# First attention: probabilities turned by an ordinary product with the identity instead of by a PE transpose

## The chip, the cores and the metric

The kernel runs on one core of one Trainium2 chip. The metric is the device time of one execution in microseconds (us); lower is better. In the profile PE is TensorE (PEld its loads of weights), DVE is VectorE, ACT is ScalarE, POOL is GpSimd and SP is SyncE, which issues most transfers.

## The reference

Two transformer blocks on 256 tokens of 1024 features, in float32. The first has a mixer (attention with 8 heads beside a gated convolution) and a mixture of 32 experts; the second has a linear recurrence beside an attention with 16 heads, and an MLP. The change lies in the attention of the first block:

```python
def one_block(args):                      # a block of 128 queries
    qn_b, qr_b, s0 = args
    s = (jnp.einsum('bqhd,bkhd->bhqk', qn_b, k_nope) + jnp.einsum('bqhr,bkr->bhqk', qr_b, k_rope)) * ATTN_SCALE
    mask = (k_idx[None, :] >= PAD_FRONT) & (k_idx[None, :] <= q_idx[:, None])
    s = jnp.where(mask[None, None], s, NEG_INF)
    p = jax.nn.softmax(s, axis=-1).astype(v.dtype)
    return jnp.einsum('bhqk,bkhd->bqhd', p, v)
```

8 heads, 96 features of a query and a key (64 + 32 turned by position), 64 of a value; 16 meta tokens and 256 tokens are keys, the 256 tokens are queries.

## The kernel before

The program is written out by hand, engine by engine, and the engines meet at named semaphores. Weights come in slabs of 1 MB into a ring of 12 slots. ACT and DVE split each unit of a slab (128 x 1024) into a high and a low part (`WH`, `WL`, four buffers; the semaphore `unit_split`), PE multiplies with both and then frees the buffer (`unit_used`). A slot takes its first expert weights when the last unit of its slab is split.

First attention runs over steps n = 0 to 15, which are 8 heads times 2 blocks of queries (`qt` = n % 2). An even step has 144 keys (16 meta and 128), an odd step 272. Buffers alternate by n % 2. In each step:

- PE, `scores(n + 2)` (L1758): a product over 96 rows, into PSUM bank 4 or 5.
- DVE, `negative_max(n + 1)` (L1181 to L1183): adds the causal mask, takes the row maximum; then L1193 and L1194 divide the probabilities of step n by their sum (`prob_ready`).
- ACT, `exps(n + 1)` (L709): the exponent, with its sum; then L722 and L724 copy the turned probabilities of step n from PSUM to SBUF (`probT_ready`).
- PE, the turns (L1785, L1786): the probabilities of step n, queries by keys, become keys by queries in bank 6 or 7. An even step has one turn of 128 x 128 and one of 128 x 16, an odd step two of the first kind and one of the second (`prob_turned`).
- PE, `weigh_values(n - 1)` (L1770, L1771): the values of 128 keys, once or twice, and of the 16 remaining keys.

PE works in the order in which it is written: scores(n + 2), turns(n), values(n - 1). So each of its waits is for something that another engine has had about a step's time to do. `exps(n)` waits for the turns of n - 2. After step 15 PE waits for ACT's copies of the attention's result (`aT_ready`), and then multiplies with the output weights: the mix units, L1814 to L1816 in the helper `triple_rows`. Other names below: L1836 turns rows of tokens; L2088, L2121 and L2102 are the scores, turns and values of second attention, which has a like loop over 16 steps with two heads in each; L533 and L388 are where transfers are issued.

```python
for n in range(HEADS * TT):
    qt = n % TT
    if n + 2 < HEADS * TT:
        scores(n + 2)
    pe.wait_ge(ev("prob_ready"), n + 1)
```

Of the kernel before, what the change touches and what calls it, by code (L numbers as in the profile page):

```python
# [16 lines left out]
P = 128  # L17
# [3 lines left out]
META = 16  # L21
# [92 lines left out]
def build(nc, A, out):  # L114

    ctx = ExitStack()
    with ctx:
        def sb(name, shape, dt=F32):
            return ctx.enter_context(nc.sbuf_tensor(name, shape, dt))
# [31 lines left out]
        def ev(name):  # L151

            if name not in made:
                made[name] = ctx.enter_context(nc.semaphore(name))
            return made[name]
# [17 lines left out]
        ident = sb("ident", [P, P])  # L173
# [22 lines left out]
        ps = ctx.enter_context(nc.psum_tensor("ps", [P, 8, 512], F32))  # L196

        def ar(a, n, **k):
            return big[:, ARENA + a:ARENA + a + n]
# [17 lines left out]
        prob = ar(7424, 2 * T).rearrange("p (b t) -> p b t", b=2)  # L217
# [29 lines left out]
        def z(g):  # L247
            return big[:, Z0 + g * SLAB:Z0 + (g + 1) * SLAB].rearrange("p (c t) -> p c t", c=DC)

        zx, zg, zq, zk, _, _, zc, zi = (z(g) for g in range(8))  # L250
        g_lru, g_att, vtok2, ple = slot_tok(5), slot_tok(2), slot_tok(4), slot_tok(1)
        gain_final = big[:, Z0 + 7 * SLAB:Z0 + 7 * SLAB + D]
# [154 lines left out]
        def _(sp):  # L407
# [6 lines left out]
            for i, (name, _) in enumerate(SLABS1):  # L414
                if i >= RING:
                    sp.wait_ge(ev("unit_split"), LAST1[i - RING] + 1)
                s = slot((i + SHIFT1) % RING)
                if name in cols:
                    a, b = cols[name]
                    dst, src = s[:, 0:DC * (b - a)].rearrange("p (c n) -> p c n", c=DC), pcn(w_in)[:, :, a:b]  # L420
                elif name == "uq":
                    dst, src = s[:, 0:2 * 768].rearrange("p (c n) -> p c n", c=2), pcn(w_uq)
                elif name == "ukv":
                    dst, src = s[:, 0:D], w_ukv
                elif name.startswith("or"):
                    a = 256 * int(name[2:])
                    dst, src = s.rearrange("p (c n) -> p c n", c=2), pcn(w_out[a:a + 256, :])
                elif name in ("shg", "shu"):
                    w = A["w_sh_gate" if name == "shg" else "w_sh_up"][0]
                    dst, src = s.rearrange("p (c n) -> p c n", c=DC), pcn(w)  # L430
                else:
                    dst, src = s.rearrange("p (c n) -> p c n", c=2), pcn(A["w_sh_down"][0])
                sp.dma_start(dst, src).then_inc(slab1(i)[0], 16)
                if name == "or3":

                    sp.wait_ge(ev("split_low"), SP_AT["pre_mix"] + DC)
                    for k in range(TT):
                        sp.dma_start(h_tok[:, k, :], A["x"][0, k * P:(k + 1) * P, :]).then_inc(ev("h_loaded"), 16)
# [23 lines left out]
            def slot_empty(m):  # L462

                before_m = m - RING2
                if before_m == SLAB_LRU:
                    sp.wait_ge(ev("gates_done"), DC)
                else:
                    done = max(k for k, (mm, _) in enumerate(UNITS2) if mm == before_m) + 1
                    sp.wait_ge(ev("unit_split"), U1 + done)
# [1165 lines left out]
        def _(pe):  # L1635
            mm = nc.tensor.matmul
# [35 lines left out]
            tr = nc.tensor.transpose  # L1672
# [59 lines left out]
            b = uk % NB  # L1732
# [20 lines left out]
            def scores(n):  # L1753
                h, qt = divmod(n, TT)
                keys = META + (qt + 1) * P
                if n >= 2:
                    pe.wait_ge(ev("exp_done"), n - 1)
                mm(ps[:, 4 + n % 2, 0:keys], qcat[0:QD, h, qt * P:(qt + 1) * P], kcat[0:QD, h, 0:keys],  # L1758
                   start=True, stop=True).then_inc(ev("scores"), 1)
# [3 lines left out]
            def weigh_values(n):  # L1763
                h, qt = divmod(n, TT)
                pe.wait_ge(ev("probT_ready"), n + 1)
                o = ps[(h % 2) * VD:(h % 2 + 1) * VD, h // 2, qt * P:(qt + 1) * P]
                vs = slice(h * VD, (h + 1) * VD)
                pT = probT(n % 2)
                for k in range(qt + 1):
                    mm(o, vtok[:, k, vs], pT[:, k, :], start=k == 0, stop=False, skip_group_check=True)  # L1770
                mm(o, vtok[0:META, qt + 1, vs], pT[0:META, 2, :], start=False, stop=True, skip_group_check=True)\  # L1771
                    .then_inc(ev("att_out"), 1)
# [6 lines that stand above are left out]
                if n >= 2:  # L1779
                    pe.wait_ge(ev("probT_ready"), n - 1)  # L1780
                elif n == 1:
                    pe.wait_ge(ev("std_ready"), NORM_NO["conv"] + 1)
                b = n % 2
                for k in range(qt + 1):
                    tr(ps[:, 6 + b, k * P:(k + 1) * P], prob[:, b, k * P:(k + 1) * P], ident[:])  # L1785
                tr(ps[0:META, 6 + b, 3 * P:4 * P], prob[:, b, (qt + 1) * P:(qt + 1) * P + META], ident[:])\  # L1786
                    .then_inc(ev("prob_turned"), 1)
                if n:
                    weigh_values(n - 1)
            weigh_values(HEADS * TT - 1)  # L1790
# [207 lines left out]
            with pe.If(more > 0):  # L1998
                pe.wait_ge(ev("ffn_summed"), TT)
                pe.sem_inc(ev("o_by_tensor"), 1)  # L2000
                with pe.Fori(0, ROUNDS - 1) as r:
                    with pe.Fori(0, QUADS) as q:
                        b = r * QUADS + q
# [105 lines left out]
            for n in range(HEADS2):  # L2109
                j, qt = divmod(n, TT)  # L2110
# [146 lines left out]
```

## Time and profile before

| | |
|---|---|
| median of 3 runs | 1003.41 us (1003.18 to 1003.44) |
| the profiled execution | 1000.23 us, of which its span is 998.5 us |
| PE busy | 847.7 us, 85% of the span |
| DVE busy | 522.6 us, 52% |
| ACT busy | 384.9 us, 39% |
| granted TensorE clock, mean over the span | 0.911 of 2.4 GHz |
| read from HBM | 203.87 MB, 205 GB/s over the span |

A line of the profile names the engine, the line of the kernel, what is written and read, and the shape: `96*128 96x272` is a weight tile of 96 rows and 128 columns against 272 moving columns. `xN` counts records. An engine's row in 40 slices gives tenths of busy time in slices of 25 us each; PEclk there is the granted clock in tenths. In a table by stretch the columns are the stretch and its length, busy time of each engine with its number of records, then the granted clock, the DMA engines' share and GB/s. The chain of waits gives start, time until the next link, and what ran. A matmul's modelled end lies after the start of the next one, since they are pipelined, so in the timeline the time between two starts is what a matmul costs.

### The profile page before, as it was taken

How to read it: one execution, taken by the hardware profiler on the slowest of the kernel's cores; microseconds unless marked ns; L12 is line 12 of the kernel's file. 1: busy time of each engine (PE TensorE's matmuls, PEld its weight loads, DVE VectorE, ACT ScalarE, POOL GpSimd, SP SyncE). 2: the span in 40 equal slices, each digit the busy share in tenths (PEclk: the TensorE clock that was granted, in tenths of full speed). 3: DMA queues.
4: the chain of work that ended last, by engine and by line, in shares of the span. 5: the costliest groups of instructions: out<-in, count | busy, mean ns of one | idle time of the engine just before them, and what ended most of it. 6: DMA issues, size and time to landing. Idle time of an engine off the chain costs nothing.

```text
span 998.5 us, 13335 instructions
## 1 busy us (share of the span) xinstructions
PE 847.7 (85%) x5425; PEld 660.3 (66%) x5425; DVE 522.6 (52%) x857; ACT 384.9 (39%) x637; POOL 37.0 (4%) x101
## 2 busy tenths in 40 slices
PE   6878699878966777566799999769999999999975
PEld 3778455666633444223798987447787899889964
DVE  1669842464010101202675589885577666666655
ACT  3533533362100001003545575554534544444334
POOL 3000000000101101010000000000000000000000
PEclk9899855889988978888899999799999999999988
DMA  9941100614999999999750835206555556555101
GB/s 275 387 139 50 43 1 27 243 47 163 373 423 422 419 422 420 421 420 375 228 184 27 337 130 211 92 1 232 169 172 173 167 201 199 185 169 192 62 0 43
DMA packets 78287, 205.82 MB, mean 206 GB/s; under 512 B 8120, under 2 KB 51264, under 8 KB 65936
## 3 DMA queue, kind: packets, MB, share of 16 engines
q1 hardware_dynamic: 67584, 151.46, 42.4%
q0 software_dynamic: 8016, 53.27, 13.1%
q8 instruction: 45, 0.74, 0.3%
q10 hardware_dynamic: 2624, 0.20, 0.2%
q14 instruction: 18, 0.15, 0.0%
HBM read 203.87 MB, written 1.05 MB: 205 GB/s over the span
## 4 chain that ended last, share of the span: by engine, by line
PE 61%; DMA 16%; DVE 16%; ACT 4%; issue 2%; POOL 0%; SPq 0%; ACTq 0%; DVEq 0%
DMA big<-in_w_gate 14%; PE ps L1814 8%; PE ps L1815 8%; PE ps L1816 8%; PE ps L1640 7%; PE ps L1642 7%; PE ps L1641 7%; PE ps L1910 4%; DVE WL L1017 2%; DMA big<-in_w_in 2%; PE ps L1665 1%; DVE big L1499 1%; PE ps L1758 1%; PE ps L1770 1%; DVE WL L1009 1%
## 5 line engine op out<-in xcount | busy, mean ns | idle before, releaser
L1017 DVE TENSOR_TENSOR WL<-big,WH 128x1024 fp32r<-128x1024 f32 x154 | 186.7, 1224 | 110.6 <-ACT WH L601 109.2
L601 ACT ACTIVATE WH<-big 128x1024 fp32r<-128x1024 f32 x154 | 160.7, 1054 | 87.2 <-PE ps L1816 86.7
L1640 PE MATMUL ps<-XH,WH 128*128 128x256 f32 (+1 forms) x640 | 185.1, 289 | 5.9 <-DVE XL L1032 5.2
L1642 PE MATMUL ps<-XH,WL 128*128 128x256 f32 (+1 forms) x640 | 182.7, 285 | 0.0
L1641 PE MATMUL ps<-XL,WH 128*128 128x256 f32 (+1 forms) x640 | 182.6, 285 | 0.0
L1640 PEld LDWEIGHTS ps<-XH,WH 128*128 128x128 f32 x640 | 123.0, 192 | 9.1 <-issue 6.3
L1641 PEld LDWEIGHTS ps<-XL,WH 128*128 128x128 f32 x640 | 123.3, 193 | 0.8
L1642 PEld LDWEIGHTS ps<-XH,WL 128*128 128x128 f32 x640 | 123.2, 193 | 0.0
L1910 PE MATMUL ps<-big 128*32 128x256 f32 x1024 | 79.3, 478 | 51.5 <-DMA big<-in_w_gate 34.1
L1814 PE MATMUL ps<-WH,XH 128*128 128x512 f32 x256 | 103.9, 406 | 11.6 <-DVE WL L1009 5.0
L1910 PEld LDWEIGHTS ps<-big 128*32 128x32 f32 x1024 | 44.2, 137 | 88.9 <-issue 79.3
L1815 PE MATMUL ps<-WH,XL 128*128 128x512 f32 x256 | 101.9, 398 | 0.0
L1816 PE MATMUL ps<-WL,XH 128*128 128x512 f32 x256 | 101.6, 397 | 0.0
L1350 DVE TENSOR_TENSOR big<-big,ps 128x256 f32<-128x256 f32 x8 | 3.4, 421 | 130.7 <-ACT big L799 130.7
L1814 PEld LDWEIGHTS ps<-WH,XH 128*128 128x128 f32 x256 | 49.6, 194 | 25.5 <-DVE WL L1009 5.4
L1814 PE MATMUL ps<-WH,HH 128*128 128x512 f32 x144 | 57.1, 396 | 1.7 <-DVE HL L1596 1.7
L1815 PE MATMUL ps<-WH,HL 128*128 128x512 f32 x144 | 56.4, 392 | 0.0
L1816 PEld LDWEIGHTS ps<-WL,XH 128*128 128x128 f32 x256 | 49.3, 193 | 10.7
L1816 PE MATMUL ps<-WL,HH 128*128 128x512 f32 x144 | 56.1, 390 | 0.0
L1815 PEld LDWEIGHTS ps<-WH,XL 128*128 128x128 f32 x256 | 49.4, 193 | 9.9
L1009 DVE TENSOR_TENSOR WL<-big,WH 128x1024 fp32r<-128x1024 f32 (+1 forms) x39 | 40.2, 1044 | 21.8 <-ACT WH L592 21.5
L959 ACT ACTIVATE HH<-big 128x256 fp32r<-128x256 f32 x32 | 13.4, 417 | 76.2 <-DVE big L1593 76.2
(354 smaller groups left out, 1132.4 us busy)
## 6 DMA issues: line engine op xcount, KB each, us to landing
big<-in_w_in SPq DMA_DIRECT2D x35, 1024.0 KB, 9.2
big<-in_w_gate SPq DMA_DIRECT2D x16, 1024.0 KB, 16.5
big<-in_w_up SPq DMA_DIRECT2D x16, 1024.0 KB, 18.5
big<-in_w_gate POOLq DMA_DIRECT2D x16, 1024.0 KB, 18.7
big<-in_w_up POOLq DMA_DIRECT2D x16, 1024.0 KB, 20.7
big<-in_w_down SPq DMA_DIRECT2D x16, 1024.0 KB, 18.5
big<-in_w_down POOLq DMA_DIRECT2D x16, 1024.0 KB, 20.8
big<-in_w_mlp_up SPq DMA_DIRECT2D x16, 1024.0 KB, 5.5
```

The source lines that it names most:

```text
L601: s.activation(dst, src, ACT.Copy).then_inc(ev("unit_high"), 1)
L959: s.activation(HH[:, f % 2, :], zx[:, f % 2, :], ACT.Copy).then_inc(ev("relu_high"), 1)
L1009: v.tensor_tensor(dst, src, h.bitcast(F32), ALU.subtract).then_inc(ev("unit_split"), 1)
L1017: v.tensor_tensor(dst, src, h.bitcast(F32), ALU.subtract).then_inc(ev("unit_split"), 1)
L1499: ins = v.tensor_tensor_scan(out=cum(b)[:, h, S - keys:S][:, ::-1], data0=omb[:, h, ::-1], data1=ones[:, 0:1].to_broadcast([P, keys]), ini ...
L1640: mm(o, h, rh, start=first, stop=False, skip_group_check=skip)
L1641: mm(o, h, rl, start=False, stop=False, skip_group_check=skip)
L1642: return mm(o, l, rh, start=False, stop=last, skip_group_check=skip)
L1814: mm(o, h, WH[:, b, w], start=first, stop=False, skip_group_check=skip)
L1815: mm(o, l, WH[:, b, w], start=False, stop=False, skip_group_check=skip)
L1816: return mm(o, h, WL[:, b, w], start=False, stop=last, skip_group_check=skip)
L1910: last = mm(ps[j * CAP:(j + 1) * CAP, 1, up * FF:(up + 1) * FF], x(c)[:, j * CAP:(j + 1) * CAP], slot(first_slot + j)[:, c * FF:(c + 1) * FF],
```

## The change

The turns on L1785 and L1786 become ordinary products: the same operands (probabilities as the weights, the identity as what moves), the same place in PSUM, the same semaphore. The order of PE's instructions and every wait stay as they are. In what follows a turn is the transpose of one tile, a product the matmul that replaces it.

```diff
                 for k in range(qt + 1):
-                    tr(ps[:, 6 + b, k * P:(k + 1) * P], prob[:, b, k * P:(k + 1) * P], ident[:])
-                tr(ps[0:META, 6 + b, 3 * P:4 * P], prob[:, b, (qt + 1) * P:(qt + 1) * P + META], ident[:])\
-                    .then_inc(ev("prob_turned"), 1)
+                    mm(ps[:, 6 + b, k * P:(k + 1) * P], prob[:, b, k * P:(k + 1) * P], ident[:], start=True, stop=True)
+                mm(ps[0:META, 6 + b, 3 * P:4 * P], prob[:, b, (qt + 1) * P:(qt + 1) * P + META], ident[:],
+                   start=True, stop=True).then_inc(ev("prob_turned"), 1)
```

## Rows read from the trace of the kernel before

**Rows 1.** The page: PE's total, and three lines in 40 slices.
```profile
PE 847.7 (85%) x5425; PEld 660.3 (66%) x5425; DVE 522.6 (52%) x857; ACT 384.9 (39%) x637; POOL 37.0 (4%) x101
...
PEclk9899855889988978888899999799999999999988
DMA  9941100614999999999750835206555556555101
```

**Rows 2.** Busy time by stretch: one pair of steps, the stage, the first mix units.
```profile
149.37:155.31 5.94, 5.94 (x20) 3.43 (x19) 2.45 (x10) 1.89 (x8) 0.00 (x0) 0.50 0.00 0
124.30:170.40 46.10, 46.01 (x148) 25.99 (x148) 18.43 (x76) 15.93 (x64) 0.00 (x0) 0.50 0.00 1
...
171.80:175.50 3.70, 3.70 (x9) 2.94 (x10) 0.00 (x0) 0.65 (x2) 1.08 (x3) 0.50 0.73 263
```

**Rows 3.** The chain of waits through one pair of steps (start, us, what).
```profile
143.50 1.20 PE ps L1758 x2
144.71 0.43 PE ps L1785 x2
145.13 0.21 PE ps L1786
145.35 0.62 PE ps L1770 x2
145.97 0.61 PE ps L1771 x2
146.58 0.78 PE ps L1758 x2
147.36 0.21 PE ps L1785
147.57 0.21 PE ps L1786
147.79 1.04 PE ps L1770 x4
148.83 0.61 PE ps L1771 x2
```

**Rows 4.** Waits of SP's and POOL's queues, 120 to 240 us (total, times, longest).
```profile
SPq L388 <- DVE WL L1009: 118.0, 3, 82.3
...
POOL big L388 <- DVE WL L1009: 28.3, 2, 18.4
```

**Rows 5.** The chain of waits behind the last values.
```profile
170.41 1.39 issue
```

**Rows 6.** Groups by form on PE, 124.3 to 170.4 us (records, busy us, mean ns).
```profile
L1770 PE MATMUL ps<-XT,big 128*64 128x128 f32 x32 | 8.9, 435 | 0.0
...
L1785 PE MATMUL ps<-ident,big 128*128 128x128 f32 x24 | 8.7, 430 | 0.0
L1786 PE MATMUL ps<-ident,big 128*16 128x128 f32 x16 | 6.7, 421 | 0.0
...
L1770 PE MATMUL ps<-big 128*64 128x128 f32 x16 | 5.5, 448 | 0.0
```

**Rows 7.** By stretch: second attention twice, then before and after 482.7 us.
```profile
636.30:646.60 10.30, 9.34 (x44) 5.18 (x44) 8.94 (x20) 6.42 (x14) 0.00 (x0) 0.50 0.00 1
646.60:672.00 25.40, 17.68 (x150) 10.44 (x148) 23.50 (x50) 14.34 (x35) 0.00 (x0) 1.00 0.00 1
479.80:482.70 2.90, 2.84 (x14) 2.84 (x15) 0.92 (x3) 0.94 (x4) 0.00 (x0) 0.50 1.09 328
482.80:486.20 3.40, 3.18 (x26) 2.97 (x24) 3.26 (x8) 3.40 (x8) 0.00 (x0) 1.00 0.77 188
```

**Rows 8.** Timeline of PE around 482 us (start, us, instruction, idle before).
```profile
479.86 3.35 PE L1836 MATMUL ps<-ident,big 128*128 128x128 f32 x16 [10.07 <-DVE big L1415]
```

**Rows 9.** Timeline of PE in second attention.
```profile
658.93 0.44 PE L2102 MATMUL ps<-big 128*64 128x128 f32 x4
659.30 0.49 PE L2088 MATMUL ps<-big 64*128 64x128 f32 x4
```

## Prediction

> **What bounds the kernel now.** I read the page first. PE is busy 85% of the span, and its clock line stands at 5 tenths in the two slices from 125 to 175 us, where the line of the DMA engines is at 0 [rows 1]. This is the first attention, the stage that is changed. I then read the chain of waits through it: from 126 us to 170 us it runs almost wholly on PE, from one matmul to the next, with no step on DVE, ACT or DMA. The table by stretch agrees: from 124.3 to 170.4 us PE is busy 46.01 of 46.10 us, DVE 18.43, ACT 15.93, and the granted clock is 0.50 throughout, the lower of its two levels (1.2 GHz of 2.4) [rows 2]. So PE sets the time, at half its clock, and what is added to PE is added to the stage.
>
> The chain shows the rhythm [rows 3]. One pair of steps (an odd step, then an even one) takes 5.94 us: scores 1.20, two wide turns 0.43, the narrow one 0.21, values 0.62 and 0.61; then scores 0.78, turns 0.21 and 0.21, values 1.04 and 0.61. Sixteen steps make eight pairs.
>
> Does the rest shift with the end of this stage? SP's queue waited 118.0 us in three waits and POOL's 28.3 us for the split of weight units, which stands still until PE frees a buffer behind attention, and the DMA engines moved 0 to 1 GB/s meanwhile [rows 2, 4]. The expert transfers, which keep the DMA line at 9 from 250 to 475 us [rows 1], therefore start in step with the end of attention. Behind the last values comes a gap of 1.39 us for ACT's copies [rows 5], then the mix units. I count the shift one for one.
>
> **The change, part by part.** It takes away 40 turns (24 wide, 16 narrow, one record each) and puts 40 products in their place [rows 6]. Nothing moves in any engine's order, and no wait and no DMA is added. What does a product of 128 columns cost? The values are such products, in the same fp32. Eight even and eight odd steps hold 8 + 16 = 24 of them on line 1770, and the trace has 32 + 16 = 48 records [rows 6]: an fp32 product is issued as two passes, a turn as one. The pass costs the same either way: two further passes on line 1770 take 1.04 - 0.62 = 0.42 us, and two turns 0.43 [rows 3]. So each turn gains one pass of 0.213 us at the half clock. The weight load of the second pass lies under the first, as it does between the passes of line 1770, which follow without a gap; were it not so, each would cost as much as a change of shape, 0.62 - 0.43 = 0.19 us more. Below, the bound is nothing added (one pass after all).
>
> At the half clock that is 40 x 0.213 = **8.5 us** more. Nothing hides it: PE has 0.09 us idle in the stage. With unhidden loads it would be 16 us, which I count unlikely. A page of the Trainium skill speaks against the change: Perfetto Trace Analysis, section Transposes, says to use the transpose for a transpose and not an ordinary matmul. The rows agree as far as the price of a pass goes, and by that page alone the kernel would lose the 8.5 us.
>
> **The clock is the other term.** PE's stream in a pair is now 4.59 us of passes (5 turns; 10 of values at 0.213; scores 1.39) and 1.35 us of changes between groups of unlike shape, in which nothing streams. With the product it is 5.65 us of passes and the same 1.35, 7.0 us in all, and the passes added use all 128 rows of the array, unlike the scores (96) and half the values (16). The engine gets fuller; could the clock go up? Second attention has the same kind of loop: PE was busy 9.34 of 10.30 us at 0.50, and then the clock rose and stayed at 1.00 for 25.4 us in which PE was busy only 17.68 [rows 7]. So such a loop can lift the clock, and once lifted it is held by much less work than first attention offers. First attention as it is sits below what lifts it, not far below as I judge, since second attention looks little fuller.
>
> Does a turn count less than a product for the clock? Before 482.7 us PE ran sixteen turns and nothing else, at 0.50, and the clock then went to 1.00 [rows 7, 8]. Turns do lift it. The Trainium skill (TensorE: Matmul & The Clock Gate, section Part 4: PE-mode transpose) says that the full clock does not engage for transposes, which are not counted as PE being busy in the same way. The sixteen turns speak against that. Were the page right, the change would raise the counted work more than I say, and the rise below would be the surer.
>
> What a rise gives. From 124.3 to 170.4 us are 46.1 us; with the product at the half clock 54.6. At the full clock the passes of a pair take 5.65 / 2 = 2.83 us. The changes between shapes shrink less: in second attention two passes and such a change take 0.37 us at 1.00 (658.93 to 659.30) [rows 9], so 0.37 - 0.22 = 0.15 against 0.19. That gives 1.35 x 0.8 = 1.08, and a pair of 3.9 us; the ends are 3.5 (all halves) and 4.2 (changes stay). DVE (2.45) and ACT (1.89 us of work in a pair) [rows 2] still fit below it, and what they add in waits I put at 1 us over the stage, an estimate, for the first and last steps. With the rise t us into the stage it lasts t + (54.6 - t) x 0.56 = 30.6 + 0.44 t. I take t = 6: 33.2 us, 12.9 less than now. The first mix units, 3.7 us at 0.50 today [rows 2], would start at 1.00 and save 1.8. Less the 1 us: 13.7, say **14 us** saved. The profiled execution took 1000.23 us, 3.2 less than the median of 1003.41; I put the change on the median: **989.4 us**. Its own range is 984 (t = 0, a pair of 3.5) to 994 (t near 16).
>
> **The rivals.**
> *The clock stays at 0.50.* For it: 46 us of PE without a gap did not lift it, and the turns already counted. Against it: the passes go from 77% to 81% of the pair and gain full height. Price +8.5: 1012. It decides if the fuller loop is still not enough. Chance 0.33.
> *It rises late,* more than 16 us in. Each us later costs 0.44; the gain is used up at t of about 35 to 40. Times 994 to 1010. Chance 0.12, half of it faster, half slower.
> *The change does nothing to the end:* the product goes out in one pass, or the shift is taken up by the expert transfers. The two records of every product on line 1770 speak against the first, the waits of SP and POOL against the second. 1003.4, chance 0.05.
> *Forecast:* the clock rises in the first third. 0.50.
>
> **Numbers.** A measurement of this kernel can tell about 0.2% (2 us) from no change. Faster: 0.50 + 0.06 + 0.01 = 0.57; same 0.04; slower 0.33 + 0.06 = 0.39. Both signs hold much, so the range reaches from the forecast to the first rival: 986 to 1013.
>
> **What would show it.** In the profile after: 48 and 32 records where there were 24 and 16; the stage at 0.50 with a pair of 7.0 us, then at 1.00 with one near 3.9; the end of attention at about 157 us in place of 170, or 179 if the clock stays; SP's and POOL's waits shorter or longer by the same. It would be wrong if a clock that has risen falls back within the stage, if loads show as gaps between the two passes, or if the fast loop turned out to wait for DVE's max or ACT's exponent, whose time no clock of PE's changes.

## The result: the time and the profile after

The changed kernel takes 1013.8 us (median of 4 runs, 1012.9 to 1016.15) beside 1003.29 us before; the ratio is 1.0105, 95% interval 1.008 to 1.0131. It is slower by 10.5 us. The forecast was 989.4 us with a range up to 1013, so it had the wrong sign, and the time lies just outside the range. Now and then an execution falls into a slower state (one of the kernel before took 1594.82 us, one of burst_turns 1596.41, one of burst_one 998.31), and the medians and ratios below leave such executions out.

By stretch, the changed kernel: one pair of steps, the stage, the first mix units. They answer to [rows 2].

```profile
146.25:153.47 7.22, 7.22 (x25) 4.41 (x25) 2.45 (x10) 1.77 (x8) 0.00 (x0) 0.50 0.00 0
121.90:179.20 57.30, 56.74 (x188) 34.19 (x188) 18.87 (x78) 15.70 (x65) 0.00 (x0) 0.50 0.00 1
180.70:186.70 6.00, 6.00 (x14) 4.71 (x15) 0.00 (x0) 0.60 (x2) 1.03 (x2) 0.50 0.85 329
```

The granted clock (third number from the end) is 0.50 through the whole stage: the rise that the forecast stood on did not come. A pair takes 7.22 us in place of 5.94. The chain of waits of the changed kernel through that pair, link by link, against [rows 3]:

```profile
146.25 1.20 PE ps L1758 x2
147.45 0.85 PE ps L1785 x4
148.30 0.54 PE ps L1786 x2
148.84 0.62 PE ps L1770 x2
149.46 0.61 PE ps L1771 x2
150.07 0.78 PE ps L1758 x2
150.85 0.43 PE ps L1785 x2
151.28 0.54 PE ps L1786 x2
151.82 1.05 PE ps L1770 x4
152.86 0.61 PE ps L1771 x2
```

Scores and values are as they were. The wide products take 0.85 and 0.43 us where the turns took 0.43 and 0.21: one further pass of 0.213 each, as the prediction had it. The narrow ones take 0.54, not 0.43. The timeline of the changed kernel shows why.

```profile
147.88 0.42 PE L1785 MATMUL ps<-ident,big 128*128 128x128 f32 x1
148.23 0.13 PEld L1786 LDWEIGHTS ps<-ident,big 128*16 128x16 f32 x2 [0.23 <-issue]
148.23 0.61 PE L1786 MATMUL ps<-ident,big 128*16 128x128 f32 x2
```

The narrow product starts 0.35 us after the last wide pass and not 0.21: its weights are loaded only then (the row of PEld, its idle time before it given as "issue"), so a gap stands there as between the groups of unlike shape in [rows 3]. In the kernel before, the weights of the narrow turn are loaded under the last wide one, and it starts 0.21 us after it:

```profile
144.50 0.63 PE L1785 MATMUL ps<-ident,big 128*128 128x128 f32 x2
144.72 0.14 PEld L1786 LDWEIGHTS ps<-ident,big 128*16 128x16 f32 x1
144.93 0.42 PE L1786 MATMUL ps<-ident,big 128*16 128x128 f32 x1
```

The second pass of the narrow product comes a little sooner, and 0.11 us is left of the gap. In sum 40 x 0.213 = 8.5 and 16 x 0.11 = 1.8, together 10.3 us. From the first score to the last value, the start of the first record to that of the last, the stage takes 58.87 us in place of 48.11, 10.8 more. The other 0.4 us stand in its first and last steps, where the order of instructions isn't yet, or no longer, that of the steady part.

Behind it, SP's and POOL's queues wait longer for the same thing, as [rows 4] would have it after a longer stage:

```profile
SPq L388 <- DVE WL L1009: 127.7, 3, 92.6
...
POOL big L388 <- DVE WL L1009: 66.9, 3, 36.9
```

At the head of second attention the same instructions stand 10.4 us later than before (at 641.4 in place of 631.0 us), so the shift went through the expert transfers one for one. The profiled execution lies 14.3 us above the profiled one of before, and the other 4 us are those of second attention, in which the clock was down for 37.5 us this time, where it was down for 10.3 in [rows 7]:

```profile
644.10:681.60 37.50, 34.10 (x166) 19.52 (x166) 30.36 (x63) 20.64 (x46) 1.08 (x2) 0.50 0.02 8
```

Over the profiled kernels, this one included, second attention takes between 41.5 and 46.0 us with the same code, and the runs of one kernel spread by some us with it. So in what follows the stage is read in the trace, and the median only says how much of it arrives.

### The profile page after: what moved, and what is told of

It is laid out like the page before. It is cut to its first block, busy times and chain, and to the rows that moved or that the text cites. A ratio compares the mean times of both kernels' runs of the same rounds, so it can differ in the third digit from the quotient of the medians.

```text
span 1012.8 us, 13415 instructions
## 1 busy us (share of the span) xinstructions
PE 867.9 (86%) x5465; PEld 674.4 (67%) x5465; DVE 523.4 (52%) x857; ACT 384.9 (38%) x637; POOL 37.2 (4%) x101
## 4 chain that ended last, share of the span: by engine, by line
PE 64%; DMA 15%; DVE 14%; ACT 4%; issue 3%; POOL 0%; SPq 0%; ACTq 0%; DVEq 0%
DMA big<-in_w_up 15%; PE ps L1814 8%; PE ps L1815 8%; PE ps L1816 8%; PE ps L1640 7%; PE ps L1642 6%; PE ps L1641 6%; PE ps L1910 4%; DVE WL L1017 2%; PE ps L1889 1%; PE ps L1758 1%; PE ps L1770 1%; DVE XT L1459 1%; PE ps L2088 1%; PE ps L2121 1%
## 5 line engine op out<-in xcount | busy, mean ns | idle before, releaser
L1816 PEld LDWEIGHTS ps<-WL,XH 128*128 128x128 f32 x256 | 49.6, 194 | 10.8
```

The source lines that it names most:

```text
L1816: return mm(o, h, WL[:, b, w], start=False, stop=last, skip_group_check=skip)
```

## The experiments

Fourteen kernels. The stage is the time from the first score to the last value of first attention, a pair the distance of two odd steps in its steady part, both from the trace. The kernels ran in four sessions, each beside the kernel before: wide_only to narrow_full (before: 1001.46 us), burst_turns to r_products (1001.99), tall_products to burst_r_turns (1001.11), and the last two (1002.51). The kernel before differs by up to 2.2 us from session to session, so medians are compared with the one of their own session; the ratio does so, and it isn't always the quotient of the two medians. Stage, pair and clock are those of one profiled execution of each kernel. In each of the nine profiles marked 0.50 the clock was at 1.00 when the stage began and fell 1.9 to 2.4 us later.

| kernel | median us | ratio to before (95%) | stage us | pair us | clock in the stage |
|---|---|---|---|---|---|
| before | 1003.29 | | 48.11 | 5.94 | 0.50 |
| the change | 1013.80 | 1.0105 (1.008 to 1.0131) | 58.87 | 7.23 | 0.50 |
| wide_only | 1007.57 | 1.0059 (1.0043 to 1.0076) | 53.45 | 6.59 | 0.50 |
| narrow_only | 1007.67 | 1.0065 (1.0034 to 1.0095) | 53.48 | 6.59 | 0.50 |
| turns_twice | 1012.29 | 1.0108 (1.0089 to 1.0127) | 56.50 | 7.01 | 0.50 |
| narrow_full | (see text) | | 56.86 | 7.01 | 0.50 |
| burst_turns | 986.53 | 0.9830 (0.979 to 0.9869) | 32.49 | 3.49 | 1.00 from 124.9 to 152.2 |
| burst_products | 991.12 | 0.9885 (0.9852 to 0.9919) | 36.71 | 4.07 | 1.00 from 125.3 |
| r_turns | 998.74 | 0.9967 (0.9944 to 0.9989) | 44.13 | 5.41 | 0.50 |
| r_products | 1000.32 | 0.9979 (0.9954 to 1.0004) | 45.28 | 5.52 | 0.50 |
| tall_products | (see text) | | 35.15 | 3.79 | 1.00 from 129.0 |
| fuller_products | 994.38 | 0.9932 (0.9908 to 0.9956) | 40.38 | 4.52 | 1.00 from 128.6 |
| burst_one | 984.09 | 0.9812 (0.9771 to 0.9853) | 31.00 | 3.49 | 1.00 from 124.7 |
| burst_r_turns | 982.42 | 0.9799 (0.9771 to 0.9827) | 29.71 | 3.39 | 1.00 from 119.3 to 150.0 |
| fuller_low | 1019.19 | 1.0165 (1.0122 to 1.0209) | 65.70 | 8.08 | 0.50 |
| turns_more | 992.32 | 0.9889 (0.9848 to 0.9929) | 41.87 | 4.29 | 1.00 from 137.4 |

### What a product costs: four kernels

**wide_only**, against before:

```diff
-                    tr(ps[:, 6 + b, k * P:(k + 1) * P], prob[:, b, k * P:(k + 1) * P], ident[:])
+                    mm(ps[:, 6 + b, k * P:(k + 1) * P], prob[:, b, k * P:(k + 1) * P], ident[:], start=True, stop=True)
```

> Only the 24 wide turns become products; the 16 narrow ones stay turns. Theory of passes and shapes: each product adds one pass of 0.213 us at the half clock, 24 x 0.213 = 5.1 us, and no gap stands between the wide product and the narrow turn if the gap of 0.11 us seen with the change belongs to a narrow product; if it belongs to a change from a product to another width, 16 x 0.11 = 1.8 us come on top (6.9). Rival theory, that the product as such and not its second pass is dear: the price would not be in step with the number of passes. Clock at 0.50 through first attention in both. Whole kernel 1003.3 + 5.1 to 6.9 = 1008.4 to 1010.2 us.

The pair grew by 0.65 us, which is three passes (0.64), so no gap stands between a wide product and a narrow turn.

**narrow_only**: the narrow turn alone becomes a product, as in the change.

> Only the 16 narrow turns become products. Theory of passes and shapes: 16 x 0.213 = 3.4 us, and the 0.11 us gap in front of each stays if it is the narrow product that cannot have its weights loaded ahead: 16 x 0.32 = 5.2 us. If the gap needs a product before it, 3.4 us alone. Whole kernel 1006.7 to 1008.5 us.

The pair grew by 0.65 us again, now for two products: 0.32 each, 0.213 for the pass and 0.11 for the gap. The gap belongs to the narrow product, be it a wide turn or a wide product that stands before it. The two halves add up: 5.34 + 5.37 = 10.71 us in the stage, against 10.76 for the change.

**turns_twice**, against before: both turn lines issued twice.

```diff
                 for k in range(qt + 1):
                     tr(ps[:, 6 + b, k * P:(k + 1) * P], prob[:, b, k * P:(k + 1) * P], ident[:])
+                    tr(ps[:, 6 + b, k * P:(k + 1) * P], prob[:, b, k * P:(k + 1) * P], ident[:])
```

> The kernel before with each of the 40 turns issued twice, so that PE makes as many passes as with the products, but all in transpose mode. The result is the same. If the price is the pass alone: 40 x 0.213 = 8.5 us, and no gap between wide and narrow, so 1.8 us less than the change: about 1011.8 us. If the array's clock took turns for less work than products, nothing differs, since the clock is at 0.50 in both. A rival that the product has a price of its own beyond the pass would leave this run well under the change by more than 1.8 us.

7.01 is 5.94 + 5 x 0.213: a second turn costs what the second pass of a product costs, and there is no gap. That the product has a price beyond its second pass and the narrow one's gap is ruled out. The median lies 10.8 us above that of before, where the stage grew by 8.4; second attention took 3.1 us more in this profile.

**narrow_full**, against the change:

```diff
-                mm(ps[0:META, 6 + b, 3 * P:4 * P], prob[:, b, (qt + 1) * P:(qt + 1) * P + META], ident[:],
+                mm(ps[:, 6 + b, 3 * P:4 * P], prob[:, b, (qt + 1) * P + META - P:(qt + 1) * P + META], ident[:],
```

> The changed kernel, with the narrow product widened: its weight tile is 128 columns that end with the 16 remaining keys, not those 16 alone. The rows that are then copied are of other keys, so the output is not the reference's. It keeps the number of passes (80) and takes away the change of width between the wide and the narrow product. If the gap of 0.11 us is due to that change, 16 x 0.11 = 1.8 us less than the change, about 1012.0 us; if it is due to the second product's weights being loaded late whatever their width, no difference (1013.8 us).

With weights of equal width the pair is 7.01 us, 0.22 less than with the change: the gap is gone. It came from the change of width from 128 to 16 columns in front of a narrow product; in front of a narrow turn the same change costs nothing. The median, 4482 us, can't be compared: with other attention values the kernel runs its overflow rounds, which it needs only when an expert gets more tokens than it has room for, and 3936 us lie between the two attentions in place of 461.

### What an extra burst of work at the head of the stage does

In the profile of the kernel before, the clock is at 1.00 when the stage begins, at 121.9 us, and falls at 124.3, when PE has waited 1.5 us for the first exponents. In the stretch ahead of the fall PE is busy 1.17 of 3.40 us:

```profile
120.90:124.30 3.40, 1.17 (x5) 0.54 (x4) 3.03 (x7) 0.44 (x2) 0.00 (x0) 1.00 0.00 0
```

**burst_turns**, against before:

```diff
             scores(0)
             scores(1)
+            for _ in range(2):
+                mm(ps[:, 3, :], ones[:], vtok[:, 0, :], start=True, stop=True)
```

> The kernel before, with two extra products of 128 x 512 (four passes) written into a PSUM bank that is not yet in use, placed behind the first two scores of first attention, where PE idles 1.5 us until the first exponent is done. Their result is never read. Theory: the clock falls at the start of the stage because PE runs dry there, and once at 1.00 it would be held by the loop, as second attention holds it. Then the stage runs at 1.00: a pair of steps about 3.5 us in place of 5.94, attention 14 to 16 us shorter, whole kernel about 988 us. Rival: the loop of first attention holds no clock, or it falls later all the same: within 2 us of 1003.3, or part of the gain.

The busy time by stretch: the burst, then the rest of the stage.

```profile
120.90:124.80 3.90, 3.90 (x7) 2.31 (x8) 3.03 (x9) 1.05 (x4) 0.00 (x0) 0.50 0.00 0
124.90:152.10 27.20, 26.08 (x145) 15.22 (x143) 17.61 (x72) 14.95 (x61) 0.00 (x0) 1.00 0.00 1
```

In this profile the clock was at 0.50 already when the scores and the burst began, at 120.9 us. PE ran without a gap for 3.90 us, the clock went to 1.00, and the loop of turns held it there for 27.2 us. The stage lost 15.6 us and the kernel 15.5. So the loop that 46 us at 0.50 had not lifted holds the clock once something else has lifted it. The burst need not find the clock down: in the profile of burst_r_turns below it was at 1.00 from 119.3 us, before the stage began, and stayed there.

**burst_products**: the same two lines in the changed kernel.

> The changed kernel with the same two extra products behind the first two scores. If the clock is held at 1.00 a pair takes about 3.9 to 4.1 us (in place of 7.2), the 40 second passes cost 40 x 0.11 = 4.4 us at the full clock, and the kernel is 4 to 5 us above the run with turns and extra products, about 993 us. Rival, that the clock falls all the same: 1013.8 us.

Here a pair is 4.07 us; at the full clock the change costs 0.58 us a pair, 4.2 us in the stage and 4.6 in the median, less than half of its 10.5 at the lower clock.

**burst_one**: one such product in place of two.

> The kernel before with one extra product (128 x 512, two passes) behind the first two scores in place of two. If it is only PE's dry stretch at the head of the stage that has to be filled, half of it still leaves a gap of about 0.7 us: the clock then stays at 0.50, a pair at 5.94 us and the time at 1002 us, or within 1 us. If any work there is enough, it is as with two: pairs of 3.5 us and about 987 us.

My expectation was wrong: one is enough, and it saves 1.5 us of the stage besides. It had reckoned with a burst at the full clock. In this profile the clock was at 0.50 at that point, the burst of one took 1.71 us, and PE went on without a gap until the clock had risen. One of its 4 runs was at 998.31 us, the others at 982.64 to 984.47, so it may not catch every time; that run was not profiled.

### Rounded operands

**r_turns**, against before:

```diff
+        prob_r = sel_flat[:, 0:2 * T].rearrange("p (b t) -> p b t", b=2)
+        ident_r = sel_flat[:, 6 * P:7 * P]
...
-                v.tensor_scalar(prob[:, b, 0:keys], prob[:, b, 0:keys], small[:, 10 + b:11 + b], None, ALU.mult)\
+                v.tensor_scalar(prob_r[:, b, 0:keys], prob[:, b, 0:keys], small[:, 10 + b:11 + b], None, ALU.mult)\
...
-                    tr(ps[:, 6 + b, k * P:(k + 1) * P], prob[:, b, k * P:(k + 1) * P], ident[:])
+                    tr(ps[:, 6 + b, k * P:(k + 1) * P].bitcast(F32R), prob_r[:, b, k * P:(k + 1) * P], ident_r)
```

> The kernel before, but DVE writes the scaled probabilities as rounded fp32r (into the space of the keys' high and low parts, free by then) and the turns are of fp32r with an fp32r identity. The probabilities lose low bits. If a turn of fp32r streams one column a cycle, where fp32 takes two, 40 x 0.107 = 4.3 us less at the half clock: about 999 us. If a turn takes the same whatever the type, 1003.3 us.

5.41 = 5.94 - 5 x 0.107: an fp32r turn takes half the time of an fp32 one.

**r_products**: fp32r operands in the changed kernel, with `mm` in place of `tr`.

> The changed kernel with the same fp32r probabilities and identity: an fp32r product goes in one pass of one cycle a column, as in the rest of the kernel (0.107 us for 128 columns at the half clock). Theory of passes: 40 x 0.107 = 4.3 us less than before, plus up to 16 x 0.11 = 1.8 us for the change of width: 999 to 1001 us, and 12 to 15 us under the change. Rival, that a product with the identity is dear whatever its type: near 1013.8 us. The probabilities lose low bits.

One pass of 0.107 us, like the fp32r turn, plus the gap of the narrow product, 2 x 0.055 a pair: 5.52. In fp32r the product loses to the turn by the gap alone, so most of what makes the change dear is fp32's second pass. The median can't be told from that of before. The chain of waits of r_turns shows the narrow turn at 0.11 us:

```profile
150.13 0.21 PE ps L1788 x2
150.35 0.11 PE ps L1789
```

**burst_r_turns**: both ideas together, in case they beat both kernels.

> The two extra products and the fp32r turns together. The clock as with the extra products alone; each of the 40 turns takes 0.055 us in place of 0.109 at the full clock, so up to 2.2 us less than the run with the extra products alone, if PE and not DVE or ACT still sets a pair of 3.49 us: about 985 us, ratio to before near 0.981. If another engine sets it by then, no difference. The probabilities lose low bits.

982.42 us, ratio 0.9799 (0.9771 to 0.9827): 2% under before and 3% under the change. A pair is 3.39 us, 0.10 less than with fp32 turns where the passes would give 0.27: in the steady part PE is busy 17.89 of 19.00 us, where in burst_turns it was 19.59 of 20.00 (130 to 150 us), so PE no longer sets all of it.

```profile
130.00:149.00 19.00, 17.89 (x107) 11.16 (x107) 12.99 (x53) 10.91 (x45) 0.00 (x0) 1.00 0.01 2
```

### What was missing for the clock to rise

The forecast had the second pass lift the clock. **fuller_products**, against the change:

```diff
                     mm(ps[:, 6 + b, k * P:(k + 1) * P], prob[:, b, k * P:(k + 1) * P], ident[:], start=True, stop=True)
+                mm(ps[:, 6 + b, 2 * P:3 * P], prob[:, b, 0:P], ident[:], start=True, stop=True)
```

> The changed kernel with one more wide product in each step, 16 in all, into unused columns of the bank of turned probabilities; its result is never read. Two passes of 0.213 us more in a step at the half clock, full height, no further change of shape: a pair of 7.23 + 0.85 = 8.08 us, and 1013.8 + 6.8 = 1020.6 us if the clock stays at 0.50. If a somewhat fuller loop lifts the clock, the rest runs at about 4.5 us a pair and the kernel ends between 993 and 1005 us. This tells whether the forecast failed by little, on how full PE is, or altogether.

Sixteen useless products more, and the stage is 18.5 us shorter than with the change. The kernel is 6.7 us faster than before, where the change was 10.5 slower: 17.2 us between them. Two stretches, of which the first begins 2 us ahead of the stage:

```profile
118.50:128.50 10.00, 8.47 (x26) 5.18 (x24) 6.96 (x22) 1.83 (x8) 0.00 (x0) 0.50 0.00 0
128.70:162.70 34.00, 32.52 (x202) 21.85 (x202) 15.24 (x62) 15.07 (x62) 1.18 (x3) 1.00 0.01 1
```

One of its 10 runs was at 1003.4 us, the others at 992.66 to 995.82.

**tall_products**, against the change:

```diff
-                mm(o, vtok[0:META, qt + 1, vs], pT[0:META, 2, :], start=False, stop=True, skip_group_check=True)\
+                mm(o, vtok[:, 0, vs], pT[:, 0, :], start=False, stop=True, skip_group_check=True)\
```

> The changed kernel, with the value product over the 16 remaining keys replaced by one over the first 128 keys (L1771), so that it uses all 128 rows and its shape is that of the product before it. The attention's result is another one. In the stage the number of passes and of moving columns is the same. Theory that height counts: with only the scores (96 rows) short of full height, and the change of shape of 0.19 us a step gone as well, the clock is lifted within the stage and a pair falls from 7.23 to about 4 us. Rival, that nothing in such a loop lifts the clock: 0.50 throughout and a pair of 7.23 - 0.38 = 6.85 us. It is read from the stage alone, since the experts' part may take another course with other values.

The clock rose as well, in the one profile there is. (Its median of 4458 us has the overflow rounds in it, as above, and can't confirm it.)

```profile
122.20:129.00 6.80, 6.29 (x20) 4.20 (x21) 3.57 (x15) 2.80 (x12) 0.00 (x0) 0.50 0.00 0
129.00:155.00 26.00, 25.85 (x165) 18.19 (x165) 15.25 (x62) 11.92 (x53) 0.00 (x0) 1.00 0.01 2
```

Both kernels made PE fuller and what streams taller at once, the second through the change of shape that it takes away (a pair is 3.79 us, 0.28 less than in burst_products with as many passes). **fuller_low** adds the same passes as fuller_products over 16 rows, against the change:

```diff
+                mm(ps[(h % 2) * VD:(h % 2 + 1) * VD, 6 + n % 2, 2 * P:3 * P], vtok[0:META, qt + 1, vs], pT[0:META, 2, :],
+                   start=True, stop=True, skip_group_check=True)
```

> The changed kernel with one more product in each step as in the run with one more wide product, same passes and same moving columns, but over 16 rows of the array in place of 128 (a second copy of L1771's product, into unused columns, never read), next to L1771, so without a further change of shape. If only the time in which PE streams matters, the clock is lifted as with the wide one: a pair near 4.5 us and about 994 us. If the height of what streams matters, the clock stays at 0.50: a pair of 7.23 + 0.85 = 8.08 us and about 1002 + 10.5 + 6.8 = 1019 us.

The clock stayed down, and every pass was paid in full: a pair of 8.08 us, 1019.19 us, although PE streams for as long in a pair as in fuller_products. The theory of streaming time alone is out. But the product added here has a weight tile of 16 rows and 64 columns, the one of fuller_products 128 and 128, so rows and columns changed together. Two runs above bear on which it is: narrow_full widened 16 products from 16 to 128 columns and the clock stayed at 0.50, and tall_products raised 16 products from 16 to 128 rows at 64 columns and it rose, though with a change of shape less. They point at the rows; no run changes the rows alone.

```profile
125.00:180.00 55.00, 55.00 (x192) 35.57 (x192) 16.50 (x67) 12.55 (x57) 0.00 (x0) 0.50 0.00 1
```

**turns_more** makes the passes of fuller_products all as turns: turns_twice, and before the narrow turns

```diff
+                for _ in range(2):
+                    tr(ps[:, 6 + b, 2 * P:3 * P], prob[:, b, 0:P], ident[:])
```

> The kernel before with every turn issued twice and two further wide turns in each step, so that PE makes as many passes, of the same height, as in the run with products and one more wide product, but all of them in transpose mode. If turns count for the clock as products do, it is lifted as there: about 4.3 to 4.5 us a pair and 990 to 996 us. If turns count for less, it stays at 0.50, with a pair of 7.01 + 0.85 = 7.86 us and about 1018 us.

```profile
123.80:137.30 13.50, 13.22 (x48) 9.06 (x48) 5.82 (x24) 3.75 (x18) 0.00 (x0) 0.50 0.00 1
137.50:163.50 26.00, 26.00 (x172) 18.05 (x172) 12.78 (x52) 11.04 (x47) 0.00 (x0) 1.00 0.01 1
```

The added turns lift the clock too: beside turns_twice, which stayed at 0.50, this kernel has two wide turns more in each step and nothing else. Whether a turn counts as much as a product is not shown; the rise came 9 us later than in fuller_products in this one profile. By their times (990.34 to 994.85 us) all 4 runs had it. Nor does the state at the head of the stage decide: in fuller_products the clock was at 0.50 when the stage began, but here and in tall_products it was at 1.00, fell, and rose again within the loop.

## Why the prediction was wrong

- *PE sets the stage, at 0.50, and its shift goes through one for one:* right. The stage grew by 10.8 us, the head of second attention moved by 10.4, the median by 10.5.
- *A product adds one pass of 0.213 us:* right, shown by the halves of the change and by turns_twice. (Of the ten passes of values in a pair four are over 16 rows, not half, as the prediction says; its sums don't use that.)
- *The weight load of the second pass is hidden, at 0.19 us more if not:* right for the second pass. But the term left out another place: the narrow product behind a wide one pays a change of width, 0.11 us x 16 = 1.8 us, which turns don't pay. The first rival's price should have been 10.3 and not 8.5 us; with it that rival gives 1013.7 us, which is what was measured, 0.8 us above the upper end of the range.
- *With the product the clock rises in the first third of the stage:* the step that failed. It rested on "not far below as I judge, since second attention looks little fuller". That it was not far below is shown: 16 further wide products lift it, and so do values of full height. But the 40 products alone did not: the clock stayed at 0.50 through the profiled stage, and by their times (1012.9 to 1016.15 us) in all 4 runs. What I passed over was that second attention is not the same kind of loop. In first attention the scores use 96 rows of the array and the last values 16, and the values 64 columns, one pass after another. Second attention runs two heads side by side: its scores are two products of 64 rows whose records start within 0.01 us of each other, its values two of 64 columns. At 0.50 eight of its passes take 1.06 us (642.82 to 643.88), where four of first attention take 1.04 [rows 3]:

```profile
642.82 1.13 PE L2102 MATMUL ps<-big 128*64 128x128 f32 x8
643.88 0.80 PE L2088 MATMUL ps<-big 64*128 64x256 f32 x2
```

So its busy time, from which I argued, hides how much of the array works at once. fuller_low shows that busy and streaming time aren't all that counts: the same passes lift nothing from a tile of 16 x 64, and lift the clock from one of 128 x 128. Which property of the tiles decides stays open, as said there. That the first rival's time came so close is no merit of the forecast; it had the lesser chance.

- *Turns count for the clock:* right (turns_more), against the Trainium skill (TensorE: Matmul & The Clock Gate, section Part 4: PE-mode transpose), if not shown to count in full. Transposes alone made up what was added there, and the clock went from 0.50 to 1.00. The rule on the other side, that of the Trainium skill in Perfetto Trace Analysis, section Transposes, held: the product lost to the turn in fp32 at either clock (by 10.8 us of the stage at 0.50, by 4.2 at 1.00).
- *Once lifted, the loop holds it, and a pair takes 3.9 us:* shown by burst_products, with 4.07 (the narrow product's gap is in it).
- *Chances:* the rows read from the trace of before had none in which a loop with such a mix of tiles was lifted. 46 us in which PE was all but never idle and the clock stayed down was the strongest row on the question, and 0.33 was too little for it.

What stays open: why single runs of fuller_products and burst_one lay 10 to 15 us above the rest. No profile caught one. Whether their clock rose late was not seen. And rows, columns and changes of shape have not been taken apart as to what they do to the clock.

## What to carry to other kernels

In this trace an fp32 turn is one pass and an fp32 product two, so an ordinary product in place of a turn costs a pass, and here nothing came back for it; fp32r halves the turn (0.107 us in place of 0.213 at 0.50), where its rounding is allowed. If PE is busy without a gap and the clock still stands at 0.50, ask first what happens where the clock fell: one useless product in the wait at the head of this stage was worth 17 us, more than any change to the loop that keeps the result was worth alone. And before you count on a rise because another loop had one, compare not only how full PE is but the rows and columns of its tiles, and whether two of them run side by side.

## What the runs showed that I had not expected

- In front of a narrow product a change of the weights' width from 128 to 16 columns costs 0.11 us at the lower clock (0.35 us from start to start in place of 0.21, of which the next pass gives a part back); in front of a narrow turn it costs nothing.
- The same loop runs steadily at 0.50 (5.94 us a pair for 46 us) or at 1.00 (3.49 us a pair for 27 us), depending on whether PE stood idle for 1.5 us or had a useless product to do in the wait at the head of the stage.
- Adding 32 passes to the changed kernel made its stage 18.5 us shorter (fuller_products).
- Second attention takes 41.5 to 46.0 us in kernels that differ in nothing there; in the two profiles compared at the top it was at 0.50 for 10.3 us and for 37.5 us.
